# Matrix memory of a streaming-encoder layer: its small native fp32 products as split high and low products

## The chip, the cores and the metric

One core of a Trainium2 chip. The metric is the device time of one launch in microseconds, as the median of several runs of the same program.

## The reference

One layer on 256 tokens of width 2048, all in fp32. The part that matters here is the matrix memory (mLSTM), eight heads, keys and queries of 128, values of 256:

```python
logw = jnp.where(causal, bc[..., :, None] - bc[..., None, :] + ic[..., None, :], -jnp.inf)
...
w_intra = jnp.exp(logw - m_t[..., None])
...
sc = jnp.einsum('bhtd,bhsd->bhts', qc, kc) * w_intra
num = w_inter[..., None] * jnp.einsum('bhtd,bhde->bhte', qc, c_mat) + jnp.einsum('bhts,bhse->bhte', sc, vc)
den = w_inter * jnp.einsum('bhtd,bhd->bht', qc, n_vec) + jnp.sum(sc, axis=-1)
h = num / jnp.maximum(jnp.abs(den), jnp.exp(-m_t))[..., None]
```

The reference runs this chunk by chunk with a carried matrix. The kernel computes the same sums without the carry, over all 256 tokens in two tiles of 128. Around it lie a latent attention, the gated merge of the two branches, an attention to 256 memory tokens and a gated feed-forward network.

## The kernel before, in words

All large products are split by hand. A weight block (128 x 1024, one of some 600) lands in `w_raw`; ScalarE (ACT) copies it rounded into `w_hi` (L787), VectorE (DVE) writes the remainder into `w_lo` (L1300), and TensorE (PE) makes three single-pass products of type fp32r from the parts: high by high, high by low, low by high (`by_tokens`, L323 to L325, 12 matmuls of 512 columns for a block). Four slots hold blocks. `split(pos, c)` on ACT waits until PE has used block c (`w_used`), then makes the high part of block c + 4 in the same slot; DVE's `split(pos, c)` follows with the low part. SyncE's queue loads the next block once the low part is made. Each engine works through its instructions strictly in the order in which they are written.

The matrix memory is `mlstm_pass`, once on each of PE (L526), ACT (L1044) and DVE (L1604), for four passes of two heads. Each pass carries eight weight blocks c0 to c7 of another product (the output gate's columns); the memory's own steps are placed by hand between them:

- PE: c0; then, once keys (`k_st`) and stabilisers (`m_st`) are staged, for each head the scores keys by queries, 256 and 128 columns (L536, L538); then, after the first two of DVE's `y_b` operations of the pass before (they read the same bank), ones by stabilisers, 512 columns (L542); c1 to c3; after `ml_p`, for each head three products of weights by values with 257 columns, the last column being ones (L549 to L551); c4 to c7; transposes of the result (L559).
- DVE: split 0; the arguments of the exponential into `w_ml` (L1610, L1612); split 1; the triangle mask (L1618); scores times weights (L1621), which releases PE by `ml_p`; splits 2 and 3; normalisation of the result (L1627 to L1647) with splits 4 to 6; staging of the next pass's stabilisers (`stage_m`, L1601); split 7; the low part of `y_b` (L1659).
- ACT: the sigmoid of the gate (L1032); splits 0 and 1; the exponential (L1052), ahead of which a function table is loaded; splits 2 to 4; squares and a root (L1062, L1065); splits 5 and 6; the copy of the next keys (`stage_k`, L1041); split 7; the high part of `y_b` (L1075).

These small products are native fp32 matmuls: the trace shows each as two MATMUL records and two weight loads (so x2), where a split fp32r one is one record. Ahead of the first pass DVE finishes the attention's last result (L1584), clears `m_st` (L1664) and stages the first stabilisers.

The helpers `TTo`, `TS` and `STT` are DVE's tensor_tensor, tensor_scalar and scalar_tensor_tensor; `step` issues an instruction and waits for its end.

Of the kernel before, what the change touches and what calls it, by code (L numbers as in the profile page):

```python
# [98 lines left out]
def build(nc, x, x_t, mem, mem_by_feature, positions, cols_d, mats_d, stream, out):  # L99
    ctx = ExitStack()  # L100
    with ctx:
# [10 lines left out]
        def region(name, nbytes, *plans):  # L112

            res = {}
            for plan in plans:
                with ExitStack() as s:
                    for tname, shape, dt in plan:
# [32 lines left out]
        DV1 = ML_DV + 1  # L150
# [15 lines left out]
            [("mpad", [P, zv_b // 4 + 16 * T + 5 * T], F32),  # L166
             ("sig", [P, TT, BLK], F32), ("k_st", [P, 2, T], F32), ("m_st", [P, 2, T], F32),
             ("w_ml", [P, 2, 384], F32), ("hn", [P, 2, TT, T], F32), ("junk", [P, T], F32)],
            [("mg_t", [P, KC, 2, T], F32R), ("mg_pad", [P, (zv_b + 16384 + 5120 - 32768) // 4], F32),
# [8 lines left out]
         k_tok, pe_n, pe_tok, pe_b, v_pair, pr, prt, r0_bc, sig, k_st, m_st, w_ml, hn, junk, mg_t, sgb, mg_a, mg, x_sq, yc, x_tok, ua, ub, xa, xb, h_st, r_diag, r_bc) = (  # L178
# [3 lines left out]
                            "sig", "k_st", "m_st", "w_ml", "hn", "junk", "mg_t", "sgb", "mg_a", "mg", "x_sq", "yc",  # L182
# [7 lines left out]
        r_x0, eps_x0 = tiny[:, 62:64], tiny[:, 24:26]  # L190

# [90 lines left out]
        def _(pool):  # L282
# [10 lines left out]
            for i in range(2):  # L293
                pool.dma_start(mem_raw[:, KPB * i:KPB * (i + 1), :].rearrange("p k t -> p (k t)"),
                               mem_by_feature[:, KPB * i * T:KPB * (i + 1) * T]).then_inc(sem(f"memf_landed{i}"), 16)

            pool.wait_ge(sem("mg_lo"), 2 * NBLK)
            for t in range(TT):
                pool.dma_start(x_tok[:, t, :], x[t * P:(t + 1) * P, :]).then_inc(sem(f"x_again{t}"), 16)
            for t in range(TT):  # L300
                pool.dma_start(mem_tok[:, t, :], mem[t * P:(t + 1) * P, :]).then_inc(sem(f"mem_landed{t}"), 16)
# [5 lines left out]
        def _(pe):  # L307
# [218 lines left out]
            def mlstm_pass(pos, j, bank):  # L526
# [4 lines left out]
                pe.wait_ge(sem("k_staged"), j + 1)  # L531
                pe.wait_ge(sem("m_staged"), 2 * j + 2)
                for i in range(2):
                    q_all = qk[:, bass.ds(2 * j + i, 1), :]
                    q_late = qk[:, bass.ds(2 * j + i, 1), P:T]
                    pe.matmul(ps[:, ATT + i, 0:T], k_st[:, i, 0:P], q_all, start=True, stop=True,  # L536
                              skip_group_check=True)
                    mm = pe.matmul(ps[:, ATT + i, T:T + P], k_st[:, i, P:T], q_late, start=True, stop=True,  # L538
                                   skip_group_check=True)
                if j:  # L540
                    pe.wait_ge(sem("yb_lo"), 4 * j - 2)
                mm = pe.matmul(ps[:, ATT + 2, :], ones[:], m_st[:].rearrange("p h t -> p (h t)"), start=True,  # L542
                               stop=True).then_inc(sem("ml_scored"), 1)
# [3 lines left out]
                for i in range(2):  # L547
                    v0, v1 = (v_aug[:, t, bass.ds(2 * j + i, 1), :] for t in range(TT))
                    pe.matmul(ps[:, ATT + 2 * i, 0:DV1], w_ml[:, i, 0:P], v0, start=True, stop=True)  # L549
                    pe.matmul(ps[:, ATT + 2 * i + 1, 0:DV1], w_ml[:, i, P:T], v0, start=True, stop=False)  # L550
                    mm = pe.matmul(ps[:, ATT + 2 * i + 1, 0:DV1], w_ml[:, i, T:T + P], v1, start=False, stop=True)  # L551
# [227 lines left out]
        def _(act):  # L779
# [9 lines left out]
            def mem_squares(t):  # L789
                act.wait_ge(sem(f"mem_landed{t}"), 16)  # L790
# [3 lines left out]
            def mem_high(i):  # L794
                act.wait_ge(sem(f"memf_landed{i // 4}"), 16)
# [241 lines left out]
            def stage_k(j):  # L1037
                act.wait_ge(sem("cv_made"), 4)
                if j:
                    act.wait_ge(sem("ml_scored"), j)  # L1040
                act.activation(k_st[:], qk[:, 2 * j + ML_HEADS:2 * j + ML_HEADS + 2, :], ACT.Copy  # L1041
                               ).then_inc(sem("k_staged"), 1)

            def mlstm_pass(pos, j, bank):  # L1044

                sigmoid_block(bank)
                for c in range(2):
                    split(pos, c)
# [990 lines left out]
```

## Time and profile before

| | |
|---|---|
| median of 3 runs | 1756.96 us (1756.79 to 1757.66) |
| the profiled execution, its time | 1757.24 us |
| its span, first to last instruction | 1755.4 us |
| PE busy | 1748.4 us, 8758 matmul records |
| PE weight loads busy | 1484.2 us |
| DVE busy | 1113.3 us |
| ACT busy | 932.8 us |
| the four passes of the matrix memory | from about 391 to 501 us of the span |

PE is one chain of matmuls through the whole span. Matmul records overlap, as their ends are modelled: the time that a matmul costs is read from the distance between starts, not from its duration. Moments below are microseconds from the start of the span.

### The profile page before, as it was taken

How to read it: one execution, taken by the hardware profiler on the slowest of the kernel's cores; microseconds unless marked ns; L12 is line 12 of the kernel's file. 1: busy time of each engine (PE TensorE's matmuls, PEld its weight loads, DVE VectorE, ACT ScalarE, POOL GpSimd, SP SyncE). 2: the span in 40 equal slices, each digit the busy share in tenths (PEclk: the TensorE clock that was granted, in tenths of full speed). 3: DMA queues.
4: the chain of work that ended last, by engine and by line, in shares of the span. 5: the costliest groups of instructions: out<-in, count | busy, mean ns of one | idle time of the engine just before them, and what ended most of it. 6: DMA issues, size and time to landing. Idle time of an engine off the chain costs nothing.

```text
span 1755.4 us, 25994 instructions
## 1 busy us (share of the span) xinstructions
PE 1748.4 (100%) x8758; PEld 1484.2 (85%) x8758; DVE 1113.3 (63%) x1541; ACT 932.8 (53%) x1262; POOL 5.6 (0%) x14
## 2 busy tenths in 40 slices
PE   9999999999999999999999999999999999999999
PEld 7888888888888888888888888888888888888887
DVE  6888876666755454545665666777666666755554
ACT  7765556656754444444664565555555555544443
POOL 0000000000000000000000000000000000000000
PEclk9999999999999999999999999999999999999999
DMA  8555454544455555556855455555555555565554
GB/s 321 189 173 173 163 170 160 165 160 150 153 178 190 192 190 191 191 192 216 308 184 189 146 168 192 191 185 187 190 187 189 186 188 185 188 200 195 191 191 155
DMA packets 90853, 329.75 MB, mean 188 GB/s; under 512 B 10128, under 2 KB 10384, under 8 KB 89776
## 3 DMA queue, kind: packets, MB, share of 16 engines
q1 hardware_dynamic: 89712, 321.96, 56.1%
q0 software_dynamic: 1088, 7.07, 1.0%
q8 instruction: 34, 0.56, 0.1%
q14 instruction: 19, 0.16, 0.0%
HBM read 326.83 MB, written 2.10 MB: 187 GB/s over the span
## 4 chain that ended last, share of the span: by engine, by line
PE 99%; DMA 0%; DVE 0%; ACT 0%; SPq 0%; issue 0%; ACTq 0%
PE ps L342 22%; PE ps L323 14%; PE ps L325 14%; PE ps L324 14%; PE ps L350 11%; PE ps L741 4%; PE ps L740 4%; PE ps L739 4%; PE ps L451 2%; PE ps L453 1%; PE ps L452 1%; PE ps L495 1%; PE ps L496 1%; PE ps L611 0%; PE ps L513 0%; DMA x_t<-in_x_t 0%
## 5 line engine op out<-in xcount | busy, mean ns | idle before, releaser
L1300 DVE TENSOR_TENSOR w_lo<-w_raw,w_hi 128x1024 fp32r<-128x1024 f32 x598 | 729.5, 1224 | 588.3 <-ACT w_hi L787 586.4
L787 ACT ACTIVATE w_hi<-w_raw 128x1024 fp32r<-128x1024 f32 x598 | 628.6, 1057 | 670.9 <-PE ps L325 334.5
L342 PE MATMUL ps<-u,w_hi 128*128 128x512 f32 x1664 | 422.1, 393 | 0.0
L342 PEld LDWEIGHTS ps<-u,w_hi 128*128 128x128 f32 x1664 | 297.9, 189 | 52.5
L323 PE MATMUL ps<-w_hi,u 128*128 128x512 f32 x608 | 242.3, 398 | 1.6 <-DVE w_lo L1337 1.4
L350 PEld LDWEIGHTS ps<-u,w_lo 128*128 128x128 f32 x1664 | 226.9, 190 | 16.4
L325 PE MATMUL ps<-w_hi,u 128*128 128x512 f32 x608 | 236.9, 390 | 0.0
L324 PE MATMUL ps<-w_lo,u 128*128 128x512 f32 x608 | 236.8, 389 | 0.0
L350 PE MATMUL ps<-u,w_lo 128*128 128x256 f32 x1664 | 231.9, 282 | 0.0
L323 PEld LDWEIGHTS ps<-w_hi,u 128*128 128x128 f32 x608 | 114.2, 188 | 27.2 <-issue 2.4
L325 PEld LDWEIGHTS ps<-w_hi,u 128*128 128x128 f32 x608 | 114.1, 188 | 24.2
L324 PEld LDWEIGHTS ps<-w_lo,u 128*128 128x128 f32 x608 | 114.3, 188 | 23.5 <-issue 1.0
L739 PE MATMUL ps<-w_hi,h_st 128*128 128x512 f32 x336 | 130.7, 389 | 0.0
L740 PE MATMUL ps<-w_lo,h_st 128*128 128x512 f32 x336 | 130.7, 389 | 0.0
L741 PE MATMUL ps<-w_hi,h_st 128*128 128x512 f32 x336 | 130.7, 389 | 0.0
L740 PEld LDWEIGHTS ps<-w_lo,h_st 128*128 128x128 f32 x336 | 63.1, 188 | 13.2
L739 PEld LDWEIGHTS ps<-w_hi,h_st 128*128 128x128 f32 x336 | 63.1, 188 | 13.1
L741 PEld LDWEIGHTS ps<-w_hi,h_st 128*128 128x128 f32 x336 | 63.1, 188 | 13.0
L323 PE MATMUL ps<-w_hi,mg_t 128*128 128x512 f32 x128 | 50.1, 392 | 0.0
L323 PE MATMUL ps<-w_hi,y_a 128*128 128x512 f32 x128 | 49.9, 390 | 0.0
L325 PE MATMUL ps<-w_hi,mg_t 128*128 128x512 f32 x128 | 49.8, 389 | 0.0
L324 PE MATMUL ps<-w_lo,mg_t 128*128 128x512 f32 x128 | 49.8, 389 | 0.0
(349 smaller groups left out, 1905.1 us busy)
## 6 DMA issues: line engine op xcount, KB each, us to landing
w_raw<-in_stream SPq DMA_DIRECT2D x600, 512.0 KB, 3.4
x_tok<-in_x SPq DMA_DIRECT2D x2, 1024.0 KB, 8.4
mem_raw<-in_mem_by_feature POOLq DMA_DIRECT2D x2, 1024.0 KB, 9.1
x_tok<-in_x POOLq DMA_DIRECT2D x2, 1024.0 KB, 7.8
mem_tok<-in_mem POOLq DMA_DIRECT2D x2, 1024.0 KB, 14.5
out<-x_tok SPq DMA_DIRECT2D x8, 256.0 KB, 3.2
x_t<-in_x_t SPq DMA_DIRECT2D x7, 256.0 KB, 5.3
w_raw<-in_stream SPq DMA_DIRECT2D x4, 256.0 KB, 4.9
```

The lines of the kernel that those rows point to most:

```text
L323: pe.matmul(o, a_hi, b_hi, start=(kc == 0), stop=False)
L324: pe.matmul(o, a_hi, b_lo, start=False, stop=False)
L325: mm = pe.matmul(o, a_lo, b_hi, start=False, stop=(kc == last_kc))
L342: mm = pe.matmul(ps[:, bank + m, :], w_hi[:, s, lo:lo + P], act[:, kc, :, :].rearrange("p h t -> p (h t)"), start=(kc == 0), stop=(kc == K ...
L350: mm = pe.matmul(ps[:, bank + m, T:2 * T], w_lo[:, s, lo:lo + P], act[:, kc, 0, :], start=False, stop=False)
L451: pe.matmul(o, a_hi, b_hi, start=(kc == 0), stop=False)
L452: pe.matmul(o, a_hi, b_lo, start=False, stop=False)
L739: pe.matmul(o, a_hi, b_hi, start=(first and kc == 0), stop=False)
L740: pe.matmul(o, a_hi, b_lo, start=False, stop=False)
L741: mm = pe.matmul(o, a_lo, b_hi, start=False, stop=(last and kc == 3))
L787: act.activation(w_hi[:, s, :], w_raw[:, s, :], ACT.Copy).then_inc(hi_made, 1)
L1300: TTo(w_lo[:, s, :], w_raw[:, s, :], w_hi[:, s, :].bitcast(F32), ALU.subtract).then_inc(lo_made, 1)
```

## The change

Every native fp32 product of the matrix memory becomes split products of type fp32r. New tiles hold rounded high parts: `q_st` and `k_st` (ACT, ahead of a pass), `v_st` (ACT, behind split 0), `w_ml_hi` (ACT, behind split 2). DVE makes the remainders in place of the originals: queries and keys (`stage_low`, behind `stage_m`), values (behind the arguments), weights (behind split 2; only this now releases PE by `ml_p`). The stabilisers are staged as high and low part; ones need no low part, so two products do. Values get 258 columns. On ACT the load of the function table is asked for ahead of split 1. Besides, `hn` gets another place, several semaphores are merged (late transfers of x and the memory tokens, DVE's own in attention and merge), and the first squares of the memory tokens come two blocks later. The diff, cut to its changed lines:

```diff
--- before.py
+++ after.py
@@ -147,7 +147,7 @@
-        DV1 = ML_DV + 1
+        DV1 = ML_DV + 2
@@ -163,10 +163,13 @@
-            [("mpad", [P, zv_b // 4 + 16 * T + 5 * T], F32),
-             ("sig", [P, TT, BLK], F32), ("k_st", [P, 2, T], F32), ("m_st", [P, 2, T], F32),
-             ("w_ml", [P, 2, 384], F32), ("hn", [P, 2, TT, T], F32), ("junk", [P, T], F32)],
-            [("mg_t", [P, KC, 2, T], F32R), ("mg_pad", [P, (zv_b + 16384 + 5120 - 32768) // 4], F32),
+            [("mpad", [P, zv_b // 4 + 16 * T], F32), ("q_st", [P, 2, T], F32R), ("npad", [P, T], F32),
+             ("sig", [P, TT, BLK], F32), ("k_st", [P, 2, T], F32R), ("m_st", [P, 2, 2, T], F32R),
+             ("w_all", [P, 2, 384], F32), ("w_hi_all", [P, 2, 384], F32R), ("v_st", [P, TT, 2, DV1], F32R), ("junk", [P, T], F32)],
+            [("v_low", [P, TT, ML_HEADS, DV1], F32R), ("qk_low", [P, 16, T], F32R), ("low_pad", [P, 13 * T], F32),
+             ("w_low", [P, 2, 384], F32R)],
+            [("hpad", [P, zv_b // 4 + 16 * T + 13 * T], F32), ("hn", [P, 2, TT, T], F32)],
+            [("mg_t", [P, KC, 2, T], F32R), ("mg_pad", [P, (zv_b + 16384 + 3072 - 32768) // 4], F32),
...
@@ -188,6 +191,11 @@
+        def q_rows(j, a=None):
+            return (qk if a is None else a)[:, 2 * j:2 * j + 2, :]
+
+        def k_rows(j, a=None):
+            return (qk if a is None else a)[:, ML_HEADS + 2 * j:ML_HEADS + 2 * j + 2, :]
@@ -292,13 +300,13 @@
-                               mem_by_feature[:, KPB * i * T:KPB * (i + 1) * T]).then_inc(sem(f"memf_landed{i}"), 16)
+                               mem_by_feature[:, KPB * i * T:KPB * (i + 1) * T]).then_inc(sem("memf_landed"), 16)
...
-                pool.dma_start(x_tok[:, t, :], x[t * P:(t + 1) * P, :]).then_inc(sem(f"x_again{t}"), 16)
+                pool.dma_start(x_tok[:, t, :], x[t * P:(t + 1) * P, :]).then_inc(sem("x_again"), 16)
...
-                pool.dma_start(mem_tok[:, t, :], mem[t * P:(t + 1) * P, :]).then_inc(sem(f"mem_landed{t}"), 16)
+                pool.dma_start(mem_tok[:, t, :], mem[t * P:(t + 1) * P, :]).then_inc(sem("mem_landed"), 16)
@@ -528,27 +536,32 @@
-                pe.wait_ge(sem("k_staged"), j + 1)
-                pe.wait_ge(sem("m_staged"), 2 * j + 2)
+                def products(o, a_hi, a_lo, b_hi, b_lo, first=True, last=True):
+                    pe.matmul(o, a_hi, b_hi, start=first, stop=False, skip_group_check=True)
+                    pe.matmul(o, a_hi, b_lo, start=False, stop=False, skip_group_check=True)
+                    return pe.matmul(o, a_lo, b_hi, start=False, stop=last, skip_group_check=True)
+
+                pe.wait_ge(sem("ml_low"), 2 * j + 2)
+                pe.wait_ge(sem("m_staged"), 4 * j + 4)
+                q_low, k_low = q_rows(j, qk_low), k_rows(j, qk_low)
...
-                    q_all = qk[:, bass.ds(2 * j + i, 1), :]
-                    q_late = qk[:, bass.ds(2 * j + i, 1), P:T]
-                    pe.matmul(ps[:, ATT + i, 0:T], k_st[:, i, 0:P], q_all, start=True, stop=True,
-                              skip_group_check=True)
-                    mm = pe.matmul(ps[:, ATT + i, T:T + P], k_st[:, i, P:T], q_late, start=True, stop=True,
-                                   skip_group_check=True)
+                    products(ps[:, ATT + i, 0:T], k_st[:, i, 0:P], k_low[:, i, 0:P], q_st[:, i, :], q_low[:, i, :])
+                    products(ps[:, ATT + i, T:T + P], k_st[:, i, P:T], k_low[:, i, P:T], q_st[:, i, P:T],
+                             q_low[:, i, P:T])
...
-                mm = pe.matmul(ps[:, ATT + 2, :], ones[:], m_st[:].rearrange("p h t -> p (h t)"), start=True,
-                               stop=True).then_inc(sem("ml_scored"), 1)
+                for hl in range(2):
+                    mm = pe.matmul(ps[:, ATT + 2, :], ones[:].bitcast(F32R), m_st[:, hl].rearrange("p h t -> p (h t)"),
+                                   start=(hl == 0), stop=(hl == 1))
+                mm.then_inc(sem("ml_scored"), 1)
...
-                    v0, v1 = (v_aug[:, t, bass.ds(2 * j + i, 1), :] for t in range(TT))
-                    pe.matmul(ps[:, ATT + 2 * i, 0:DV1], w_ml[:, i, 0:P], v0, start=True, stop=True)
-                    pe.matmul(ps[:, ATT + 2 * i + 1, 0:DV1], w_ml[:, i, P:T], v0, start=True, stop=False)
-                    mm = pe.matmul(ps[:, ATT + 2 * i + 1, 0:DV1], w_ml[:, i, T:T + P], v1, start=False, stop=True)
+                    for o, d, t, first, last in ((2 * i, 0, 0, True, True), (2 * i + 1, P, 0, True, False),
+                                                 (2 * i + 1, T, 1, False, True)):
+                        mm = products(ps[:, ATT + o, 0:DV1], w_ml_hi[:, i, d:d + P], w_low[:, i, d:d + P],
+                                      v_st[:, t, i, :], v_low[:, t, 2 * j + i, :], first, last)
@@ -787,12 +800,12 @@
-                act.wait_ge(sem(f"mem_landed{t}"), 16)
+                act.wait_ge(sem("mem_landed"), 32)
...
-                act.wait_ge(sem(f"memf_landed{i // 4}"), 16)
+                act.wait_ge(sem("memf_landed"), 32)
@@ -1038,19 +1051,26 @@
                     act.wait_ge(sem("ml_scored"), j)
-                act.activation(k_st[:], qk[:, 2 * j + ML_HEADS:2 * j + ML_HEADS + 2, :], ACT.Copy
-                               ).then_inc(sem("k_staged"), 1)
+                act.activation(k_st[:], k_rows(j), ACT.Copy).then_inc(sem("k_staged"), 1)
+                act.activation(q_st[:], q_rows(j), ACT.Copy).then_inc(sem("k_staged"), 1)

...
                 sigmoid_block(bank)
-                for c in range(2):
-                    split(pos, c)
+                split(pos, 0)
+                if j:
+                    act.wait_ge(sem("ml_num"), j)
+                act.activation(v_st[:], v_aug[:, :, 2 * j:2 * j + 2, :], ACT.Copy).then_inc(sem("v_staged"), 1)
+                act.preload_act_table_set("natural_log_exp_and_others")
+                split(pos, 1)

...
                 split(pos, 2)
+                for i in range(2):
+                    act.wait_ge(sem("ml_prod"), 2 * j + (i + 1))
+                    act.activation(w_ml_hi[:, i, :], w_ml[:, i, :], ACT.Copy).then_inc(sem("ml_whi"), 1)
                 split(pos, 3)
@@ -1116,8 +1136,8 @@
-                    if n == 1 and c in (2, 6):
-                        mem_squares(c // 4)
+                    if n == 1 and c in (4, 6):
+                        mem_squares(c // 5)
@@ -1554,11 +1574,11 @@
-                dve.wait_ge(sem("row_max"), 4 * it + 4)
+                dve.wait_ge(sem("row_max"), 5 * it + 4)
...
-                dve.reciprocal(tiny[:, 36:40], tiny[:, 32:36]).then_inc(sem("p_rs"), 1)
-                dve.wait_ge(sem("p_rs"), it + 1)
+                dve.reciprocal(tiny[:, 36:40], tiny[:, 32:36]).then_inc(sem("row_max"), 1)
+                dve.wait_ge(sem("row_max"), 5 * it + 5)
@@ -1598,8 +1618,16 @@
-                    TS(m_st[0:8, i, :], ncm[:], mats[0:8, 2 * j + i:2 * j + i + 1], None, ALU.mult
-                       ).then_inc(sem("m_staged"), 1)
+                    one = mats[0:8, 2 * j + i:2 * j + i + 1]
+                    TS(m_st[0:8, 0, i, :], ncm[:], one, None, ALU.mult).then_inc(sem("m_staged"), 1)
+                    dve.wait_ge(sem("m_staged"), 4 * j + (2 * i + 1))
+                    STT(m_st[0:8, 1, i, :], ncm[:], one, m_st[0:8, 0, i, :].bitcast(F32), ALU.mult, ALU.subtract
+                        ).then_inc(sem("m_staged"), 1)
+
+            def stage_low(j):
+                for i, (rows, high) in enumerate(((k_rows, k_st), (q_rows, q_st))):
+                    dve.wait_ge(sem("k_staged"), 2 * j + (i + 1))
+                    TTo(rows(j, qk_low), rows(j), high[:].bitcast(F32), ALU.subtract).then_inc(sem("ml_low"), 1)
@@ -1611,6 +1639,9 @@
+                dve.wait_ge(sem("v_staged"), j + 1)
+                two = slice(2 * j, 2 * j + 2)
+                TTo(v_low[:, :, two, :], v_aug[:, :, two, :], v_st[:].bitcast(F32), ALU.subtract)
@@ -1619,12 +1650,16 @@
                     STT(w_ml[:, i, :], ps[:, ATT + i, 0:384], ML_SCALE, w_ml[:, i, :], ALU.mult, ALU.mult
+                        ).then_inc(sem("ml_prod"), 1)
+                split(pos, 2)
+                for i in range(2):
+                    dve.wait_ge(sem("ml_whi"), 2 * j + (i + 1))
+                    TTo(w_low[:, i, :], w_ml[:, i, :], w_ml_hi[:, i, :].bitcast(F32), ALU.subtract
                         ).then_inc(sem("ml_p"), 1)
-                split(pos, 2)
                 split(pos, 3)
...

-                step(dve.tensor_copy(tiny[:, 40:44].unsqueeze(2), ps[:, ATT:ATT + 4, ML_DV:DV1]))
+                step(dve.tensor_copy(tiny[:, 40:44].unsqueeze(2), ps[:, ATT:ATT + 4, ML_DV:ML_DV + 1]))
                 step(STT(tiny[:, 56:60], tiny[:, 40:44], -1.0, tiny[:, 40:44], ALU.mult, ALU.max))
@@ -1650,6 +1685,7 @@
                     stage_m(j + 1)
+                    stage_low(j + 1)
                 split(pos, 7)
@@ -1661,8 +1697,9 @@
-            step(dve.memset(m_st[:], 0.0))
+            step(dve.memset(m_st[:].bitcast(F32), 0.0))
...
+            stage_low(0)
@@ -1671,14 +1708,13 @@
-                    TTo(mg_a[:, t, :], ps[:, GEMM + t, :], sig[:, t, :], ALU.mult).then_inc(sem("mga"), 1)
+                    TTo(mg_a[:, t, :], ps[:, GEMM + t, :], sig[:, t, :], ALU.mult).then_inc(sem("mg_read"), 1)
...
-                    TTo(mg[:, t, :], ps[:, ATT + t, :], sgb[:, t, :], ALU.mult).then_inc(sem("mgb_read"), 1)
-                dve.wait_ge(sem("mgb_read"), TT * it + TT)
-                dve.wait_ge(sem("mga"), TT * it + TT)
+                    TTo(mg[:, t, :], ps[:, ATT + t, :], sgb[:, t, :], ALU.mult).then_inc(sem("mg_read"), 1)
+                dve.wait_ge(sem("mg_read"), 2 * TT * it + 2 * TT)
@@ -1705,7 +1741,7 @@
-                        dve.wait_ge(sem(f"x_again{t}"), 16)
+                        dve.wait_ge(sem("x_again"), 32)
```

## Rows read from the trace of the kernel before

**Rows 1.** The chain that ended last, by engine: shares of the span.
```profile
PE 99%; DMA 0%; DVE 0%; ACT 0%; SPq 0%; issue 0%; ACTq 0%
```

**Rows 2.** PE's timeline: start us, us, engine line op, out<-in, count, idle before.
```profile
401.22 0.59 PE L549 MATMUL ps<-v_aug,w_ml 128*128 128x257 f32 x2
...
418.34 0.59 PE L536 MATMUL ps<-qk,k_st 128*128 128x256 f32 x2
...
418.99 0.60 PE L536 MATMUL ps<-qk,k_st 128*128 128x256 f32 x2
...
420.74 0.40 PE L324 MATMUL ps<-w_lo,u 128*128 128x512 f32 x1
...
428.70 0.59 PE L549 MATMUL ps<-v_aug,w_ml 128*128 128x257 f32 x2
...
431.53 0.40 PE L324 MATMUL ps<-w_lo,u 128*128 128x512 f32 x1
```

**Rows 3.** PE's timeline again: 256 columns single pass; transposes of 128.
```profile
29.39 0.28 PE L331 MATMUL ps<-u,w_hi 128*128 128x256 f32 x1
...
30.46 0.28 PE L331 MATMUL ps<-u,w_hi 128*128 128x256 f32 x1
...
414.72 1.03 PE L559 MATMUL ps<-mats,hn 128*128 128x128 f32 x8
```

**Rows 4.** ScalarE's timeline, end of the first pass, second pass.
```profile
413.22 0.62 ACT L1041 ACTIVATE k_st<-qk 128x512 f32<-128x512 f32 x1
...
419.96 1.06 ACT L787 ACTIVATE w_hi<-w_raw 128x1024 fp32r<-128x1024 f32 x1
423.52 1.06 ACT L787 ACTIVATE w_hi<-w_raw 128x1024 fp32r<-128x1024 f32 x1 [2.50 <-PE ps L325]
...
425.89 0.94 ACT L1052 ACTIVATE w_ml<-w_ml 128x384 f32<-128x384 f32 x2
```

**Rows 5.** VectorE's timeline over the same stretch.
```profile
415.53 0.60 DVE L1601 TENSOR_SCALAR m_st<-ncm,mats 8x256 f32<-8x256 f32 x2
416.07 1.23 DVE L1300 TENSOR_TENSOR w_lo<-w_raw,w_hi 128x1024 fp32r<-128x1024 f32 x1
417.21 1.65 DVE L1659 SCALAR_TENSOR_TENSOR y_b<-ps,cols,y_b 128x256 fp32r<-128x256 f32 x4
421.05 1.23 DVE L1300 TENSOR_TENSOR w_lo<-w_raw,w_hi 128x1024 fp32r<-128x1024 f32 x1 [2.19 <-ACT w_hi L787]
422.20 0.48 DVE L1610 TENSOR_SCALAR w_ml<-ps,a_tok 128x256 f32<-128x256 f32 x1
...
423.24 0.34 DVE L1612 TENSOR_SCALAR w_ml<-ps,a_tok 128x128 f32<-128x128 f32 x1
424.61 1.23 DVE L1300 TENSOR_TENSOR w_lo<-w_raw,w_hi 128x1024 fp32r<-128x1024 f32 x1 [1.02 <-ACT w_hi L787]
426.45 0.91 DVE L1618 TENSOR_TENSOR w_ml<-w_ml,mats 128x128 f32<-128x128 f32 x4 [0.61 <-ACT w_ml L1052]
427.27 1.02 DVE L1621 SCALAR_TENSOR_TENSOR w_ml<-ps,w_ml 128x384 f32<-128x384 f32 x2
```

**Rows 6.** Start of the first pass: PE's timeline, then VectorE's.
```profile
390.12 0.39 PE L325 MATMUL ps<-w_hi,u 128*128 128x512 f32 x1
390.77 0.67 PE L536 MATMUL ps<-qk,k_st 128*128 128x256 f32 x2 [0.26 <-DVE m_st L1601]
...
389.50 0.48 DVE L1664 MEMSET m_st<- 128x512 f32 x1
```

**Rows 7.** Groups by line and form: a subtraction of 512 elements, mean ns.
```profile
L1337 DVE TENSOR_TENSOR w_lo<-w_raw,w_hi 128x512 fp32r<-128x512 f32 x8 | 5.3, 690 | 1.1 <-ACT w_hi L830 1.1
```

**Rows 8.** The memory tokens' tile: squares, ns min/median/max, first and last start.
```profile
L791 ACT ACTIVATE mem_tok<-mem_tok x2: 1899/1900/1900, 860.9 to 871.0; 128x2048 f32<-128x2048 f32 x2
```

**Rows 9.** Mean granted clock; PE's longest wait, in total, times, longest us.
```profile
core 0: 1755.4 us, clock 1.000
...
PE ps L364 <- DVE y_a L1320: 1.5, 1, 1.5
```

More of the change, by code:

```diff
@@ L177, in build @@
         (x0_t, x0_tok, lat_tok, kpx, zi8, zf8, g8a, g8b, v_aug, qk, kpe, ncm, cos_g, sin_g, gq, gk, gp, q_tok,
-         k_tok, pe_n, pe_tok, pe_b, v_pair, pr, prt, r0_bc, sig, k_st, m_st, w_ml, hn, junk, mg_t, sgb, mg_a, mg, x_sq, yc, x_tok, ua, ub, xa, xb, h_st, r_diag, r_bc) = (
+         k_tok, pe_n, pe_tok, pe_b, v_pair, pr, prt, r0_bc, sig, q_st, k_st, m_st, w_ml, w_ml_hi, v_st, junk, v_low, qk_low, w_low, hn, mg_t, sgb, mg_a, mg, x_sq, yc, x_tok, ua, ub, xa, xb, h_st, r_diag, r_bc) = (
             zz[n] for n in ("x0_t", "x0_tok", "lat_tok", "kpx", "zi8", "zf8", "g8a", "g8b", "v_aug", "qk", "kpe",
@@ L181, in build @@
                             "v_pair", "pr", "prt", "r0_bc",
-                            "sig", "k_st", "m_st", "w_ml", "hn", "junk", "mg_t", "sgb", "mg_a", "mg", "x_sq", "yc",
+                            "sig", "q_st", "k_st", "m_st", "w_all", "w_hi_all", "v_st", "junk", "v_low", "qk_low", "w_low", "hn", "mg_t", "sgb", "mg_a", "mg", "x_sq", "yc",
                             "x_tok", "ua", "ub", "xa", "xb", "h_st", "r_diag", "r_bc"))
```

## Prediction

> **What bounds the kernel now.** I read the chain of work that ended last first: 99% of it is TensorE (PE) [rows 1]. So a microsecond counts only if PE's timeline gets longer or shorter by it; work on VectorE (DVE) and ScalarE (ACT) is free until PE waits for it. Next I read the stage that is changed, the matrix memory: four passes, each of eight weight blocks c0 to c7 with small products between them. In PE's timeline of the second pass [rows 2] the reader is to see no bracket, that is no idle time: c0 ends at 418.34, the score and stabiliser products run at once, c1 to c3 follow, then the products of weights and values at 428.70. From the second matmul of c1 (420.74) to 428.70 lie 35 matmuls of 512 columns: 0.227 us each, 2.73 a block. The only PE wait of the stage is 0.26 us in the first pass, for the stabilisers [rows 6]. Last I read what ACT and DVE do between those points [rows 4, 5], since the new products need operands that they make.
>
> **What PE saves.** The score and stabiliser products last from 418.34 until 0.227 before 420.74: 2.17 us; one head's two score products take 0.65 (418.34 to 418.99). The value products last from 428.70 until 0.227 before 431.53: 2.60, or 0.434 for each of six [rows 2]. In place of each comes three single-pass products, and for the stabilisers two. A 256-column one costs 0.119 (nine between 29.39 and 30.46) [rows 3], a 512-column one 0.227. The value products become 18 x 0.1205 (258 columns) = 2.17, a gain of 0.43. The stabilisers become 2 x 0.227 = 0.45.
> The trace has no single-pass split product of 128 columns. From below, the line through 0.119 and 0.227 gives 0.065. From above, it could cost what the whole native one costs, 0.65 - 0.434 = 0.22. The transposes of 128 columns, which also load weights for each, follow each other at (1.03 - 0.27) / 7 = 0.11 [rows 3]; they are nearest in form and I take 0.11. The scores then become 2 x (0.36 + 0.33) = 1.38. Scores and stabilisers: 1.83 against 2.17. On PE alone a pass saves 0.34 + 0.43 = 0.77 us (1.03 to 0.1 by the two bounds), four passes 3.1.
>
> **What DVE and ACT get, passes 2 to 4.** I lay the new instructions into the second pass's rows. DVE starts the next instruction some 0.08 us before the last one's end shows, so 1024 elements cost 1.15 in sequence, and 384 elements 0.47 [rows 5].
> *Ahead of the scores.* DVE's stabiliser staging at 415.53 goes from two operations to four, each pair dependent: 0.34 + 0.04 and 0.40 (a scalar_tensor_tensor of 256, 1.65 / 4) twice, 1.55 in place of 0.54. Then come two subtractions of 512, of 0.69 each [rows 7], 0.61 in sequence. ACT's second copy, 0.62 behind the one at 413.22 [rows 4], is done by 414.5 and is hidden. DVE is through at 415.53 + 1.55 + 0.61 + 0.69 = 418.4, and PE, free at 418.34, starts at 418.5: 0.15 late. Queued behind them on DVE are the split at 416.07 and the four y_b operations at 417.21. They now run from 418.3 and 419.45, and the second y_b operation ends at 420.3. PE waits for that one before the stabiliser product, since it reuses the bank: 420.4 instead of 418.5 + 1.38 = 419.9. c1 starts at 420.85, where it started at 420.51. The whole gain of the first group is gone.
> *Ahead of the value products.* This is the step that decides. DVE's chain: split 0 at 421.1 (ACT gives it at 421.05, after its sigmoid, and that doesn't move), 1.15; four arguments 1.38 (422.20 to 423.24 + 0.34); new: the values' low part, 1032 elements, 1.15, to 424.8. Split 1 needs ACT's half, which is made when PE has done c1: 423.57 + 0.29 + 1.09 = 424.95 (before: PE done with c1 at 420.51 + 2.73 = 423.23, ACT at 423.52, DVE at 424.61). Then 1.15 to 426.1, triangle 0.83, weights 0.93, split 2 1.15, to 429.0. The old chain had released PE ahead of split 2, at 427.27 + 1.02 = 428.3, 0.4 ahead of PE's 428.70. New: two subtractions of 384 behind split 2, 0.47 + 0.56: 430.05; PE starts at 430.2. So the value products start 1.5 us later than before and PE, done with c3 at 429.0, idles 1.2. Minus the 0.43 that they save: 1.06 us per pass.
> ACT's own additions are covered: the values' high part (1.06) lies in the idle time that ends at 423.52, so does the table load, which now fills the time between 423.52 + 1.06 and the exponentials at 425.89; it moves ahead of split 1, and the exponentials come at some 424.9, when DVE isn't ready for them. The weights' high copies (0.5 each) follow split 2, at 427.5 to 428.45, before DVE wants them at 429.0. If they weren't, each microsecond would count fully, since DVE waits for them. Behind the value products nothing changes, and ACT and DVE are tied to PE by the blocks used, so the delay is passed on whole: 3 x 1.06 = 3.2.
>
> **The first pass.** There is no cover here. DVE clears 1024 elements in place of 512: 0.49 becomes 0.75 (half rate added; 0.97 if doubled) from 389.50 [rows 6]. Then 1.55 for the stabilisers, and 0.61 + 0.69 for the low parts: 393.1. PE, free at 390.12 + 0.23 = 390.35, starts at 393.3, where it started at 390.77, and idles 2.9. c1 starts at 393.3 + 1.38 + 0.45 = 395.1 (before: 390.77 + 2.17 = 392.9). Split 1 reaches DVE 2.73 + 0.29 + 1.09 later, at 399.2, DVE being free; the same chain of 1.15 + 0.83 + 0.93 + 1.15 + 1.03 ends at 404.3. PE starts the value products at 404.4 and ends them at 406.6. Before they started at 401.22 [rows 2] and ended 2.60 later, at 403.8. Loss 2.8 us.
>
> **The rest.** The merged waits cost nothing: the last of the late transfers is read by squares that start at 860.9 without a wait [rows 8], and now come two blocks later; the others are issued ahead of it on the same queue. The reciprocal's semaphore, the merge pass's and 258 for 257 columns change less than 0.1 us in all.
>
> **The clock.** In this trace the mean granted clock is 1.000, the upper of the two levels, and its longest PE idle, 1.5 us [rows 9], is half of the 2.9 that I expect. The Trainium skill (TensorE: Matmul & The Clock Gate, "Part 1: The HAM clock gate") says that idle time puts the array back to half its clock, 1.2 GHz, until it has been busy again. By that the sum would have a further term, which is the third rival below; the trace can't show it.
>
> **Sum.** 2.8 + 3.2 = 6.0 us slower, 0.34%. The profiled execution took 1757.24 us (span 1755.4), 0.28 over the median of 1756.96; against the median I predict 1762.9.
>
> **Rivals.**
> 1. *Narrow products at the native price.* 128-column ones at 0.22 make the scores 2.04. In the first pass that is 0.66 more in full; in the others PE reaches the stabilisers at 420.55 instead of 420.4, 0.15 more. Together 1.1: 1764.0. For it: nothing in the trace excludes it. Against: the transposes' pitch. Chance 0.2.
> 2. *The other side: the value products don't wait for DVE.* Then PE's saving stays. Place: DVE between 421.1 and the last low part; it decides if that chain ends by 429.0, 1.05 us earlier than I lay it, as it would if subtractions of fp32 ran at half the time that the rows of 512 and 1024 show and the first pass's staging overlapped. Price: passes 2 to 4 then gain 0.34 to -0.34 ahead and 0.43 behind, near 0.1 each; the first pass loses 2.1 - 0.43 = 1.7. 1758.4, no change that counts; with the staging also hidden 1754. Against it: every such subtraction in the trace runs at one rate. Chance 0.08.
> 3. *The clock falls* in the first pass's idle time. A block at half the clock takes 2.73 us more; one block of it, partly absorbed by the wait that follows c3 (1.1): 1.6 to 2.7 more, 1764.5 to 1765.6. The page above gives that rule; here no row bears it out. Chance 0.12.
> My forecast itself: 0.55. The remaining 0.05 is for the copies on ACT coming late or anything else.
>
> **Range and chances.** My own case with its bounds (memset 0.75 to 0.97, 0.065 for a narrow product, 0.1 us on each semaphore of DVE's chain) is 1761 to 1765. The range of 8 in 10 reaches on to both dearer cases, and below halfway to the second rival: 1759.0 to 1766.5. A measurement of this kernel can tell 0.2%, 3.5 us, from no change; slower than 1760.5 are my case, rivals 1 and 3: 0.86. Within 0.2%: 0.10. Faster: 0.04.
>
> **What would show it.** PE waits named for DVE's qk_low or m_st ahead of the first score product (2.9 us once), for w_low ahead of each value product (1.0 to 1.3 us, four times), and for y_b ahead of the stabiliser product (0.3 to 0.6, three times). Value products 0.12 us apart. Pass length 28.5 in place of 27.5 (401.22 to 428.70). I am wrong if w_low's waits are absent, or if 128-column products lie 0.2 apart and move c1 by more than 0.2 in passes 2 to 4, or if the granted clock falls.

## The result, and the profile after

The changed kernel took 1765.28 us (median of 5 runs, 1763.45 to 1765.65) against 1756.96: 8.3 us slower, ratio 1.0045 with an interval of 1.0034 to 1.0055. The profiled execution took 1765.38, its span is 1763.6 against 1755.4. I had predicted 1762.9, slower by 6.0, in a range of 1759.0 to 1766.5.

First the page of the kernel after: each engine's busy time and instructions, and the shares of the chain that ended last.

```profile
PE 1750.0 (99%) x8798; PEld 1486.4 (84%) x8798; DVE 1130.0 (64%) x1569; ACT 942.1 (53%) x1278; POOL 5.7 (0%) x14
...
PE 95%; DVE 3%; ACT 1%; issue 0%; DMA 0%; SPq 0%; ACTq 0%
```

PE was 99% of the chain before [rows 1]; now 4% of it run over DVE's and ACT's work. That share isn't PE's idle time, which is some 10 us in all: at each of PE's waits the chain passes to the engine that PE waited for and follows that engine's work back. For whom PE waits, and how long, the list of its waits says (who waited, for whom, us in total, times, longest us):

```profile
PE ps L540 <- DVE w_low L1657: 3.4, 4, 0.8
PE ps L540 <- DVE qk_low L1630: 3.0, 1, 3.0
...
PE ps L554 <- DVE y_b L1695: 1.0, 3, 0.3
```

All three were named in the prediction: `w_low` four times, `qk_low` once, `y_b` three times. The other waits in the list belong to the kernel's start and were there before. PE's timeline of the second pass, in the columns of [rows 2]:

```profile
422.98 0.39 PE L333 MATMUL ps<-w_hi,u 128*128 128x512 f32 x1
423.28 0.39 PE L540 MATMUL ps<-q_st,k_st 128*128 128x256 f32 x1
...
423.75 0.22 PE L540 MATMUL ps<-q_st,k_st 128*128 128x128 f32 x1
...
424.03 0.33 PE L540 MATMUL ps<-q_st,k_st 128*128 128x256 f32 x1
...
424.61 0.27 PE L542 MATMUL ps<-q_st,qk_low 128*128 128x128 f32 x1
425.20 0.73 PE L554 MATMUL ps<-m_st,ones 128*128 128x512 f32 x2 [0.32 <-DVE y_b L1695]
...
426.00 0.39 PE L332 MATMUL ps<-w_lo,u 128*128 128x512 f32 x1
...
434.98 0.39 PE L540 MATMUL ps<-v_st,w_hi_all 128*128 128x258 f32 x1 [0.84 <-DVE w_low L1657]
435.21 0.28 PE L541 MATMUL ps<-v_low,w_hi_all 128*128 128x258 f32 x1
...
437.49 0.40 PE L332 MATMUL ps<-w_lo,u 128*128 128x512 f32 x1
```

c0 ends at 422.98 + 0.23 = 423.21; the scores start 0.07 later, take 0.75 for the first head (423.28 to 424.03) and 0.69 for the second, and PE then waits for `y_b` until 425.20. c1 to c3 end at 426.00 + 35 x 0.227 = 433.95, and the value products start at 434.98, 1.03 us later. The bracket says 0.84 of that, since it counts from the modelled end of the last matmul. The value products end at 437.49 - 0.23 = 437.26, having taken 2.28, and in the kernel before they took 2.60. From the first pass (406.40) to the second it is 28.58 us, where it was 27.48 [rows 2].

DVE's timeline over the same stretch, the answer to [rows 5]:

```profile
420.41 0.34 DVE L1622 TENSOR_SCALAR m_st<-ncm,mats 8x256 fp32r<-8x256 f32 x1
...
422.55 0.67 DVE L1630 TENSOR_TENSOR qk_low<-qk,q_st 128x512 fp32r<-128x512 f32 x1
...
424.29 1.64 DVE L1695 SCALAR_TENSOR_TENSOR y_b<-ps,cols,y_b 128x256 fp32r<-128x256 f32 x4
...
428.39 1.22 DVE L1644 TENSOR_TENSOR v_low<-v_aug,v_st 128x1032 fp32r<-128x1032 f32 x1
429.89 1.22 DVE L1320 TENSOR_TENSOR w_lo<-w_raw,w_hi 128x1024 fp32r<-128x1024 f32 x1 [0.28 <-ACT w_hi L800]
...
432.78 1.22 DVE L1320 TENSOR_TENSOR w_lo<-w_raw,w_hi 128x1024 fp32r<-128x1024 f32 x1
433.91 1.02 DVE L1657 TENSOR_TENSOR w_low<-w_all,w_hi_all 128x384 fp32r<-128x384 f32 x2
```

The reader sees the chain that the prediction laid out: staging from 420.41, the low part of the queries until 423.2, split and `y_b` behind it, no gap from 420.41 to the values' low part, a gap of 0.28 ahead of split 1 (L1320 at 429.89), split 2 at 432.78, and the weights' low parts at 433.91. These end at 434.93, 0.05 ahead of PE's start.

The start of the first pass, DVE and then PE, answers to [rows 6]:

```profile
389.83 0.91 DVE L1700 MEMSET m_st<- 128x1024 f32 x1 [0.16 <-issue]
...
392.93 0.67 DVE L1630 TENSOR_TENSOR qk_low<-qk,q_st 128x512 fp32r<-128x512 f32 x1
```

```profile
393.66 0.39 PE L540 MATMUL ps<-q_st,k_st 128*128 128x256 f32 x1 [2.96 <-DVE qk_low L1630]
...
397.62 0.63 PE L332 MATMUL ps<-w_lo,u 128*128 128x512 f32 x1
398.05 0.63 PE L333 MATMUL ps<-w_hi,u 128*128 128x512 f32 x1
```

PE idles 2.96 us. Then something comes that the kernel before did not have: from 397.62 to 398.05 two matmuls of 512 columns lie 0.43 apart, where 0.227 is normal. The view by stretches shows why (start:end, length, busy time of PE, PE's loads, DVE, ACT and POOL, then the granted clock, DMA share and GB/s):

```profile
390.00:393.60 3.60, 0.70 (x4) 0.24 (x2) 3.49 (x7) 3.57 (x6) 0.00 (x0) 1.00 0.48 148
393.60:395.00 1.40, 1.34 (x12) 1.34 (x12) 0.54 (x2) 1.40 (x2) 0.00 (x0) 1.00 0.06 12
395.00:396.00 1.00, 1.00 (x6) 0.80 (x6) 0.69 (x1) 0.98 (x2) 0.00 (x0) 0.62 0.00 0
396.00:397.00 1.00, 1.00 (x4) 0.81 (x3) 0.84 (x3) 0.69 (x1) 0.00 (x0) 0.50 0.20 25
397.00:398.00 1.00, 1.00 (x3) 0.76 (x3) 1.00 (x3) 0.00 (x0) 0.00 (x0) 0.50 0.82 283
398.00:399.00 1.00, 1.00 (x4) 0.80 (x3) 0.69 (x1) 0.00 (x0) 0.00 (x0) 0.68 0.54 217
```

The granted clock is 1.00 during the idle time itself. A mean of 0.62 from 395 to 396 puts the fall to half (the level of 1.2 GHz) at some 395.2, 1.6 us after PE has begun again; 0.68 from 398 to 399 puts the return at 398.6. Of 3.4 us half is lost, 1.7. That is the term by which the profiled execution exceeds the sum: its span is 8.2 us longer than before, of it 6.0 foreseen and 1.7 the clock. Another 0.2 lies ahead of the stage, where PE already ran that much later than in the execution before (386.50 against 386.27). The last 0.3 are small differences in the terms of the sum. The 0.2 has no cause shown: this matmul starts at 386.27 in the kernel before and 386.20 in e6, which is built on it, and at 386.43 to 387.48 in the changed kernel and the eight variants built on that one, so a small cost of the merged semaphores ahead of the stage isn't excluded.

### The profile page after: what moved, and what is told of

Read it like the earlier page. It is cut to its first block, busy times and chain, and to the rows that moved or that the text cites. A ratio compares the mean times of both kernels' runs of the same rounds, so it can differ in the third digit from the quotient of the medians.

```text
span 1763.6 us, 26120 instructions
## 1 busy us (share of the span) xinstructions
PE 1750.0 (99%) x8798; PEld 1486.4 (84%) x8798; DVE 1130.0 (64%) x1569; ACT 942.1 (53%) x1278; POOL 5.7 (0%) x14
## 4 chain that ended last, share of the span: by engine, by line
PE 95%; DVE 3%; ACT 1%; issue 0%; DMA 0%; SPq 0%; ACTq 0%
PE ps L350 22%; PE ps L331 13%; PE ps L333 13%; PE ps L332 13%; PE ps L358 11%; PE ps L754 4%; PE ps L753 4%; PE ps L752 4%; PE ps L459 2%; PE ps L461 1%; PE ps L460 1%; DVE w_lo L1320 1%; PE ps L503 1%; PE ps L504 1%; ACT w_hi L800 0%; PE ps L624 0%
## 5 line engine op out<-in xcount | busy, mean ns | idle before, releaser
L1320 DVE TENSOR_TENSOR w_lo<-w_raw,w_hi 128x1024 fp32r<-128x1024 f32 x598 | 729.3, 1224 | 576.8 <-ACT w_hi L800 574.7
```

The source lines that it names most:

```text
L1320: TTo(w_lo[:, s, :], w_raw[:, s, :], w_hi[:, s, :].bitcast(F32), ALU.subtract).then_inc(lo_made, 1)
```

## The experiments

Each difference is to runs of the kernel before on the same chip (1757.05 to 1757.23 us). The diffs are cut to the lines that matter.

**One half of the change at a time.** e1 keeps the split scores and stabilisers and makes the value products native again, without the high and low parts of values and weights:

```diff
-                        mm = products(ps[:, ATT + o, 0:DV1], w_ml_hi[:, i, d:d + P], w_low[:, i, d:d + P],
-                                      v_st[:, t, i, :], v_low[:, t, 2 * j + i, :], first, last)
...
+                    pe.matmul(o0, w_ml[:, i, 0:P], v0, start=True, stop=True)
+                    pe.matmul(o1, w_ml[:, i, P:T], v0, start=True, stop=False)
+                    mm = pe.matmul(o1, w_ml[:, i, T:T + P], v1, start=False, stop=True)
```

> Scores and stabilisers as split products, values by weights native again (no high and low parts of values and weights). My theory (PE waits for DVE's low parts, and the clock falls in the first pass's idle time): the wait of 3.0 us ahead of the first scores stays and the granted clock still falls behind it; no wait ahead of the value products. Against the kernel before: 2.1 us in the first pass, some 1.7 for the clock, 3 x 0.35 for the later passes, together +4.9: 1761.9 us. Rival, that the loss sits in the value products alone: scores and stabilisers save PE time, 1755.6 us.

e2 is the other half:

```diff
-                    products(ps[:, ATT + i, 0:T], k_st[:, i, 0:P], k_low[:, i, 0:P], q_st[:, i, :], q_low[:, i, :])
...
+                    pe.matmul(ps[:, ATT + i, 0:T], k_nat[:, i, 0:P], qk[:, 2 * j + i, :], start=True, stop=True,
+                              skip_group_check=True)
...
-                    stage_low(j + 1)
...
-            step(dve.memset(m_st[:].bitcast(F32), 0.0))
+            step(dve.memset(m_st[:, 0].bitcast(F32), 0.0))
```

> Values by weights as split products, scores and stabilisers native again (keys copied unrounded, stabilisers in one part, half the clearing). My theory: no wait in the first pass beyond 0.3 us, granted clock 1.00 throughout, a wait for w_low of some 0.9 us ahead of the value products in each of four passes, 1.25 later minus 0.43 saved: +3.3 us, 1760.3. With e1's +4.9 this gives the +8.3 of the whole change. Rival, that the clock or the first pass is all of it: 1757.0 or below.

Measured: e1 1763.11 (6 runs; ratio 1.0034, 1.0021 to 1.0047), +6.1; e2 1760.49 (10 runs; 1.0020, 1.0011 to 1.0030), +3.4, against 3.3 expected, with a clock of 1.000 in all ten. PE's waits, e1 and then e2:

```profile
PE ps L540 <- DVE qk_low L1625: 3.0, 1, 3.0
...
PE ps L554 <- DVE y_b L1683: 1.0, 3, 0.3
```

```profile
PE ps L540 <- DVE w_low L1653: 3.6, 4, 1.0
...
PE ps L548 <- DVE m_st L1621: 0.3, 1, 0.3
```

Each half has the waits that were named for it, and neither is a gain. The two losses don't add up to the whole: 6.1 and 3.4 make 9.5, the changed kernel has 8.3. The surplus is e1's, which came out 1.2 above what I expected, and the stretches of its profiled execution (1763.95, 6.9 above the kernel before) show at which term (columns as above):

```profile
390.00:394.00 4.00, 1.04 (x5) 0.60 (x4) 3.43 (x7) 3.97 (x6) 0.00 (x0) 0.90 0.40 133
394.00:395.00 1.00, 1.00 (x7) 1.00 (x6) 0.61 (x1) 0.98 (x2) 0.00 (x0) 0.50 0.05 16
...
396.00:400.00 4.00, 4.00 (x11) 3.23 (x12) 1.39 (x4) 0.00 (x0) 0.00 (x0) 0.50 0.41 131
400.00:401.00 1.00, 1.00 (x5) 0.81 (x5) 0.00 (x0) 0.00 (x0) 0.00 (x0) 0.99 0.00 0
```

Its scores start at 393.59 and run at half the clock from the first on, until 400.0: 6.4 us, so 3.2 lost, where the changed kernel lost 1.7. (The mean clock was 0.998 in this and one other run, 0.999 in four.) The first value product starts at 406.71, 5.5 after the kernel before [rows 2]; less 3.2 for the clock and 0.2 from ahead of the stage this is the 2.1 that I expected. Each later pass takes 27.86 from value product to value product, 0.38 over [rows 2], for 0.35 expected. So the clock's term was the one that was too small in this execution; in the five others no trace shows what it cost.

**Order behind the scores.** e3 moves the weights' low parts ahead of split 2, and on ACT their high copies:

```diff
-                split(pos, 2)
                 for i in range(2):
                     dve.wait_ge(sem("ml_whi"), 2 * j + (i + 1))
                     TTo(w_low[:, i, :], w_ml[:, i, :], w_ml_hi[:, i, :].bitcast(F32), ALU.subtract
                         ).then_inc(sem("ml_p"), 1)
+                split(pos, 2)
```

> The changed kernel with the weights' high copies (ACT) and low parts (DVE) ahead of split 2 in place of behind it; nothing else differs. My theory: DVE's chain to the release of PE is shorter by one split (1.15 us) less a short wait for ACT's copy; the four waits ahead of the value products (0.8 us each in the profile) go or fall under 0.15, -3.3 us against the changed kernel: 1762.0. The clock still falls. Rival, that PE then waits for split 2, which is later now: 1765 as before.

Measured 1762.27 (6 runs; 1.0031, 1.0018 to 1.0043): 3.0 less than the changed kernel, for 3.3 expected. In the list of waits `w_low` is gone; `y_b` (1.0 in three) and this one stand:

```profile
PE ps L540 <- DVE qk_low L1630: 3.0, 1, 3.0
```

This profiled execution had a clock of 1.000 and took 1760.12; compared with the one run of the changed kernel at 1.000, 1763.45, the gain is 3.3. Nothing waits for split 2.

**The clearing.** e4 contracts the stabiliser product over the eight rows that hold something and leaves the clearing out:

```diff
-                    mm = pe.matmul(ps[:, ATT + 2, :], ones[:].bitcast(F32R), m_st[:, hl].rearrange("p h t -> p (h t)"),
+                    mm = pe.matmul(ps[:, ATT + 2, :], ones[0:8, :].bitcast(F32R), m_st[0:8, hl].rearrange("p h t -> p (h t)"),
...
-            step(dve.memset(m_st[:].bitcast(F32), 0.0))
```

> The changed kernel with the stabiliser product over the 8 rows that hold stabilisers in place of 128, so that the 1024 elements need no clearing (the clearing is left out). The wait ahead of the first scores falls from 3.0 to 2.0 us. If the clock falls only after a longer idle time: it stays at 1.00, -0.95 and -1.7, 1762.7 us. If it falls here too: 1764.3 us.

A miss: 1766.20 (4 runs; 1.0048, 1.0031 to 1.0064), no faster at all. The wait did shrink, to 1.8 us, but the clock fell all the same, and for twice as long:

```profile
390.00:394.00 4.00, 2.24 (x16) 1.77 (x14) 2.47 (x6) 3.97 (x6) 0.00 (x0) 1.00 0.43 137
394.00:395.00 1.00, 1.00 (x4) 0.53 (x3) 0.41 (x1) 1.00 (x2) 0.00 (x0) 0.58 0.00 0
...
396.00:401.00 5.00, 5.00 (x14) 3.85 (x13) 2.26 (x5) 0.97 (x2) 0.00 (x0) 0.50 0.28 105
```

PE starts the scores at 392.60; half speed lasts from about 394.2 to 401.0 and costs 3.4 us. Three of the four runs were so (0.998, 1766.0 to 1766.6). The fourth, at 1.000, took 1763.64, no less than the changed kernel's run at 1.000: the 1.2 us gained in the wait must be lost elsewhere. Part of it goes to the product over 8 rows: e4's passes are 28.74 apart (407.07 to 493.29 for three), the changed kernel's 28.57 (406.40 to 492.10), which makes 0.5 in three passes. e9 below shows that form by itself; the rest, some 0.5, stays open.

**The clock by itself.** e5 lets PE compute eleven products that nobody reads in the wait ahead of the first scores:

```diff
+                if j == 0:
+                    pe.wait_ge(sem("ya_lo"), PAIRS)
+                    for i in range(11):
+                        pe.matmul(ps[:, ATT + 3, :], u[:, 0, 0, 0:P], u[:, 0, :, :].rearrange("p h t -> p (h t)"),
+                                  start=True, stop=True)
```

> The changed kernel, and PE computes 11 products of 512 columns that nobody reads (2.5 us) while it waits ahead of the first scores. The first scores start when they did, at 393.7 us or up to 0.2 later. If the fall of the clock costs what I read from the profile (3.3 us at half speed, 1.7): 1763.6 us and a mean granted clock of 1.000. If the clock costs nothing beyond the waits that follow: 1765.3 us.

e6 does the opposite to the kernel before, it adds nothing but idle time:

```diff
-            step(dve.memset(m_st[:], 0.0))
+            for _ in range(6):
+                step(dve.memset(m_st[:], 0.0))
```

> The kernel before, with DVE clearing the stabilisers six times in place of once: 5 x 0.52 = 2.6 us later, nothing else. PE idles 2.9 us ahead of the first scores. With the fall of the clock that idle time brings: +2.6 + 1.7 = 4.3 us, 1761.3. Without: +2.6, 1759.6 and a mean clock of 1.000.

e5: 1763.60 (5 runs; 1.0037, 1.0023 to 1.0051), clock 1.000 in all five: +6.4, where the changed kernel has +8.3. e6: 1762.28 (8 runs; 1.0029, 1.0019 to 1.0040), +5.1, clock 0.998 or 0.999 in all eight. From e6's list of waits:

```profile
PE ps L536 <- DVE m_st L1601: 3.6, 1, 3.6
```

and from its stretches, in the columns above:

```profile
393.00:394.00 1.00, 0.01 (x1) 0.04 (x1) 0.96 (x4) 0.61 (x1) 0.00 (x0) 0.65 0.00 0
```

Its wait grew from 0.3 to 3.6, since each further clearing took 0.66 in place of the 0.52 that I put in. So 3.3 of the median's 5.1 are idle time, and the 1.8 that remain are put down to the clock. The profiled execution (1763.42, 6.2 above) shows both: it ran at half from 393.3, ahead of the scores at 393.99, to 400.1, which costs 3.0 us of PE's time. This is the changed kernel's third term in a kernel that has nothing else of the change.

**Nothing in the way.** e7 puts each new step where its engine idled. It also has e4's product over 8 rows, and PE waits for the stabilisers only behind the score products:

```diff
@@ VectorE, mlstm_pass @@
...
-                TTo(v_low[:, :, two, :], v_aug[:, :, two, :], v_st[:].bitcast(F32), ALU.subtract)
...
                 split(pos, 1)
...
+                if j < NBLK - 1:
+                    stage_m(j + 1)
+                    stage_low(j + 1)
                 split(pos, 4)
...
                 split(pos, 6)
                 if j < NBLK - 1:
-                    stage_m(j + 1)
-                    stage_low(j + 1)
+                    stage_v(j + 1)
@@ ScalarE, mlstm_pass @@
                 split(pos, 3)
+                if j < NBLK - 1:
+                    stage_k(j + 1)
+                    stage_v(j + 1)
```

> The changed kernel with each new step put where its engine was idle: the next pass's key and query copies and value copy on ACT behind split 3, the stabilisers and the low parts of keys and queries on DVE behind the normalised result, the values' low part behind split 6, the weights' low parts ahead of split 2; no clearing; in the first pass low parts before stabilisers. My theory: passes 2 to 4 have no wait and save the 0.77 us of PE time each, 2.3; in the first pass PE waits 1.4 us for the low parts and saves 0.77; clock 1.00: 1757.0 - 2.3 + 0.9 = 1755.6 us, 0.1% below the kernel before. Rival, that split products in themselves cost PE what they save (weight loads): 1757.9 or above.

Measured 1757.72 (10 runs; 1.0005, 0.9996 to 1.0015), 2.1 above what I expected, and at the rival's number. But the cause isn't the rival's. In PE's timeline the last score product, the stabiliser product and the second matmul of c1:

```profile
420.73 0.27 PE L542 MATMUL ps<-q_st,qk_low 128*128 128x128 f32 x1
420.93 0.73 PE L554 MATMUL ps<-m_st,ones 8*128 8x512 f32 x2
...
421.93 0.39 PE L332 MATMUL ps<-w_lo,u 128*128 128x512 f32 x1
...
429.66 0.39 PE L333 MATMUL ps<-w_hi,u 128*128 128x512 f32 x1
429.97 0.39 PE L540 MATMUL ps<-v_st,w_hi_all 128*128 128x258 f32 x1
430.19 0.28 PE L541 MATMUL ps<-v_low,w_hi_all 128*128 128x258 f32 x1
```

1.20 us lie between 420.73 and 421.93, where a narrow product, two of 512 columns and the matmul after them make 0.11 + 3 x 0.227 = 0.79. And behind c3 the first value product comes 0.31 after its predecessor and its successor 0.22 behind it, in place of 0.23 and 0.12: a wait too short for a bracket, as DVE's chain ends just when PE arrives. e9 takes the first away, e8 the second. e9 has 128 rows again and clears them in the last attention pass (the line's changed operands alone):

```diff
-ones[0:8, :].bitcast(F32R), m_st[0:8, hl]
+ones[:].bitcast(F32R), m_st[:, hl]
```

> e7 with the stabiliser product over 128 rows in place of 8, and the clearing done in the last attention pass. The profile of e7 shows 1.2 us from the last score product to the second matmul of c1, where two products of 512 columns and one matmul explain 0.8. If the form of 8 rows is the cause: 0.35 to 0.4 less in each pass, passes 26.9 apart, 1756.1 us. Rival, that it is the wait for the stabilisers' semaphore: 1757.5 as e7.

1756.26 us (10 runs; 0.9996, 0.9986 to 1.0005), as expected: passes 27.0 us apart (402.38, 429.34, 456.33) where e7 has 27.3. Its PE timeline at the place of e7's first two lines and its third:

```profile
420.41 0.27 PE L542 MATMUL ps<-q_st,qk_low 128*128 128x128 f32 x1
420.52 0.68 PE L554 MATMUL ps<-m_st,ones 128*128 128x512 f32 x2
...
421.26 0.40 PE L332 MATMUL ps<-w_lo,u 128*128 128x512 f32 x1
```

The pair of products over 8 rows costs 0.3 us a pass in sequence with products of 128 rows: 0.09 ahead of it (0.20 in e7, 0.11 here) and 0.26 from its start to the second matmul behind it (1.00 and 0.74).

e8 also stages the first pass in the attention's last one, and puts the whole chain to the value products ahead of split 1, two changes at once:

```diff
                 for i in range(2):
                     dve.wait_ge(sem("ml_whi"), 2 * j + (i + 1))
                     TTo(w_low[:, i, :], w_ml[:, i, :], w_ml_hi[:, i, :].bitcast(F32), ALU.subtract
                         ).then_inc(sem("ml_p"), 1)
+                split(pos, 1)
                 split(pos, 2)
...
+            mla_pass(Pos(G_MLA + 7 * MLA_PER), 7, early=[lambda: step(dve.memset(m_st[:].bitcast(F32), 0.0)),
+                                                            lambda: stage_low(0), lambda: stage_m(0)])
```

> e7 with the stabiliser product over 128 rows again; the clearing, the first copies of keys and queries, their low parts and the first stabilisers moved into the last attention pass, where DVE and ACT idle 1.5 us for each block; and in each pass exponentials, triangle, weights and their low parts ahead of split 1 in place of behind it. My theory: PE waits nowhere in the stage, the granted clock stays at 1.00 in every run, and the whole PE saving shows: 4 x 0.77 and the 0.26 that the kernel before waited, 1757.2 - 3.3 = 1753.9 us, 0.19% below the kernel before; passes 26.7 us apart. Rival, that the split products cost PE more than the starts show: passes 27.2 apart as in e7, 1756.

1753.86 us (11 runs, 1753.56 to 1754.20; ratio 0.9982, 0.9973 to 0.9991), 3.2 below the kernel before and 11.4 below the changed kernel; the clock was 1.000. Its PE timeline at the value products of the first two passes, and the two largest waits that are left, both in the kernel's start:

```profile
400.58 0.28 PE L540 MATMUL ps<-v_st,w_hi_all 128*128 128x258 f32 x1
```

```profile
427.31 0.28 PE L540 MATMUL ps<-v_st,w_hi_all 128*128 128x258 f32 x1
```

```profile
PE ps L331 <- DVE w_lo L1362: 1.6, 2, 1.3
PE ps L372 <- DVE y_a L1345: 1.5, 1, 1.5
```

The first two value products are 26.73 apart, and the three passes from the first to the fourth (400.58 to 480.84) 26.75 on average, 0.72 less than in the kernel before (27.47). This version beats both kernels, by little: the interval reaches from 0.1 to 0.3%.

## Why the prediction was right in direction and range, and where it was short

**The bound.** PE's timeline is the kernel, and only what PE waits for counts: right. The new operations cost DVE 16.7 us and ACT 9.3 of busy time in all (1130.0 and 942.1 in place of 1113.3 and 932.8), and e8 does the same work without a wait of PE in the stage.

**What PE saves.** 258 columns at 0.1205 and 0.69 for a head's scores are borne out (435.21 and its neighbours; 424.03 to 424.61 and 0.11). Narrow products: three in 0.28 (423.75 to 424.03), so 0.09 to 0.1 each; my 0.11 was near, and the first rival (0.22) is out. The saving of 0.77 a pass that I worked out is 0.72 in e8.

**Passes 2 to 4.** I had 1.06 a pass, 28.5 us in place of 27.5; it is 1.10 and 28.58. Each wait sits where it was put: the scores 0.07 late for 0.15, `y_b` three times, `w_low` 1.03 us of PE's time for 1.2. e3 shows that the order behind the scores makes most of this part: without `w_low`'s waits the passes are 27.63 apart. e1 and e2 show the two kinds of wait each by itself. That ACT's copies are covered is shown too: DVE's subtractions at 433.91 follow split 2 without a gap. The second rival, that the value products don't wait, is out. (Its price has a slip that moves nothing: the first pass would lose 2.2 - 0.43 by the terms of the sum, not 2.1 - 0.43. Likewise my case and rivals 1 and 3 add up to 0.87, not 0.86.)

**The first pass.** The wait ahead of the scores: 2.9 foreseen, 2.96 measured; the clearing took 0.91, at the upper end of what I gave it (0.75 to 0.97). The value products end at 408.67, where they ended at 403.8: 4.9 later, of it 1.7 the clock and 0.2 from ahead of the stage, which leaves 3.0 for the 2.8 of my sum.

**The step that failed is the clock.** The prediction took the term as zero in its sum, since no row showed a lower clock, and gave a fall a chance of 0.12, at 1.6 to 2.7 us. A mean clock under 1.000 is there in four of five runs, and the one of them that was profiled lost 1.7. Without it the changed kernel took 1763.45 (one run at 1.000, +6.5) and e5 +6.4, for 6.0 predicted. The third rival had the time right (1764.5 to 1765.6; 1765.28 measured), the chance wrong, and its size by luck. It priced one block at half the clock, 2.73, and let the wait behind c3 take up as much as 1.1 of it. The trace shows a stretch of 3.4 us that ended within c1, and nothing of it was taken up: DVE's chain to the value products starts behind c1, so the wait ahead of them stayed at 0.83 in the first pass, where passes 2 to 4 have 0.84. The Trainium skill (TensorE: Matmul & The Clock Gate, "Part 1: The HAM clock gate") has the half clock after idle time. By that, the trace agrees: the granted clock reads 0.50 from 396 to 398, behind an idle time of 2.96 us. It shows besides that the fall came 1.6 us after PE had begun again. I gave it little because the trace before has a wait of 1.5 us at a clock of 1.000. That row says nothing of a wait twice as long, and in e4 the clock fell behind one of 1.8.

**The merged waits** for late transfers cost PE nothing that shows: neither kernel's list of waits names them for PE. Of DVE's merged semaphores the runs don't show it, since no run has them alone (see the 0.2 above).

## What to carry to other kernels

Splitting a native fp32 product saves PE little here: 0.07 us for 257 columns (0.434 native, 3 x 0.1205 split), 0.35 for the stabilisers' 512 (two single passes, 0.51 in e8 and e9, for the native one's 0.87), and nothing where narrow products go with it (a head's scores, 256 and 128 columns, take 0.67 to 0.69 in place of 0.65). And it needs three or four operations on other engines to make the parts, and in a kernel whose TensorE is full these decide: lay each into the consumer's chain, and find an idle place for it before counting the gain. The order of work that isn't needed yet (here a split for a later block) against work that TensorE waits for was worth 3.3 us by itself. And a single wait of TensorE of 1.8 to 3.6 us can cost a further 1.5 to 3.4 through the clock: 1.7 behind 3.0 us in the changed kernel, 3.2 behind 3.0 in e1, 3.4 behind 1.8 in e4.

## What the runs showed of the hardware that I had not expected

The clock can fall after the idle time, when PE is busy again: in the changed kernel and in e4 1.6 us after the scores had begun. In e1 and e6 it fell 0.4 and 0.7 us ahead of PE's first score product, and they ran at half from the first. And it doesn't fall in every run of one program. With PE's wait ahead of the first scores the runs went so:

| kernel | PE's wait, us | runs by mean clock 1.000 / 0.999 / 0.998 | their median times, us |
|---|---|---|---|
| e2 | 0.3 | 10 / 0 / 0 | 1760.5 |
| e9 | 1.1 | 10 / 0 / 0 | 1756.3 |
| e7 | 1.1 | 6 / 4 / 0 | 1757.5 / 1759.2 |
| e4 | 1.8 | 1 / 0 / 3 | 1763.6 / - / 1766.4 |
| changed | 3.0 | 1 / 4 / 0 | 1763.5 / 1765.3 |
| e3 | 3.0 | 1 / 2 / 3 | 1760.1 / 1761.6 / 1762.8 |
| e1 | 3.0 | 0 / 4 / 2 | - / 1762.9 / 1763.7 |
| e6 | 3.6 | 0 / 5 / 3 | - / 1762.0 / 1763.3 |

The kernel before (0.3 us), e5 (0.5, behind the eleven products) and e8 (none) were at 1.000 in every run. A fall costs 1.5 to 3.4 us, by the profiled executions and by the differences between the groups of runs, and the longest wait doesn't have the dearest fall, since it is the slow stretch that costs. From 1.8 us on most runs had one. At 1.1 us e7 had one in four of ten runs and e9 in none of ten, with the same wait ahead of the scores; they differ in the product's rows and the place of the clearing. No run of e7 at 0.999 was profiled, so where its clock fell isn't known, and ten runs each don't tell these two apart with certainty. e2's four waits of 0.9 to 1.0 us, one in each pass, brought none. What decides between a slow stretch of 3.4 us and one of nearly 7 wasn't tried.

A pair of products over 8 rows between products over 128 costs 0.3 us more than the same pair over 128 rows: 0.1 on the way into that form and 0.2 to 0.3 from there to the second product behind it. In e4, where a wait stands ahead of the pair, each pass is 0.17 longer.
